# Two-layer S5 and attention trunk: x loaded first, meta tokens turned in two transposes, B's turns between the first matmuls, one angle addition on GpSimd

## The chip, the core and the metric

One core of a Trainium2 chip runs the whole program once. The metric is the device time of that run in microseconds (us), the median of 3 runs for the kernel before; lower is better.

## What is computed

The reference runs 272 tokens (16 learned meta tokens ahead of 256 frames, 2048 wide, float32) through two layers. Layer 0 is an S5 state-space mixer, layer 1 is sliding-window attention, and a squared-ReLU MLP follows each. The change touches only the start of layer 0:

```python
h = concatenate([meta, x], axis=1)                 # 16 + 256 tokens
hn = rms_norm(h, norm_mix_gain[0])
u = hn @ w_in                                      # 2048 -> 1024
dt = exp(log_dt); lam = (a_re + i a_im) * dt
bar = exp(lam)                                     # magnitude and angle
f = (bar - 1) / (a_re + i a_im)
bb = f * (b_re + i b_im)                           # per group: 64 states x 16 channels
bu = einsum('blgc,gpc->blgp', u, bb)
x_t = bar * x_{t-1} + bu_t                         # associative scan over 272 tokens
y = Re(C x) + D * u;  z = gelu(y) * sigmoid(gelu(y) W_glu + b);  h = h + z W_out
```

The kernel runs the scan over chunks of two tokens in rotated coordinates, for which it needs the cosine and sine of 32 x 136 angles on 128 partitions (`cosb`, `sinb`).

## The kernel before, in words

Each engine has a hand-written program, and semaphores order them. TensorE's instructions run in the order in which they are written. The weights stream through a ring of four buffers, and TensorE is the engine that nearly all of the span belongs to. Tokens lie in the free dimension: `h` and `hg` (tokens times gain) are [128, 16, 272], one column block of features for each k.

The start, which is what the change edits:

- SyncE's queue (lines 580 to 613) issues a_re, a_im, log_dt (`prow`, `dtrow`), meta (`ms`, 16 rows), x block 0 (`xs`), the first piece of w_in, x block 1, b_re and b_im (`braw`), the second piece, meta once more as `ms2` (8 x 16 rows of 256), then x blocks 2 and 3 and the rest of w_in. ScalarE's queue (1066 to 1068) issues the identity (`cst`), the first gain and the step constants. GpSimd's queue issues the small vectors and, once x block 1 has landed, 16 loads of C (`craw`, 1357).
- TensorE turns the S5 parameters (660) and the gain (663), does dummy matmuls (`warm_up`, 653), and then goes through `x_unit(n)`, n = 0 to 7 (665 to 678): for each of two k one transpose of meta (675) and two of x (677). Between the units stand `in_first(k, n)` (698 to 706: four float32 matmuls, eight records in the trace, that add 512 rows of w_in to the first 256 columns of u), `b_turn(part)` (16 transposes of 32 x 128, line 686), the turn of the vectors (733) and the bias table's matmul (736), and `c_turn` (695). After `in_half(4)` come `wb_turn(0)` (769: turns of the spread B, `bp`) and three statistics matmuls (778, 780) that need `dssq`; then `in_half(5)` and `wb_turn(1)` to `(3)`, `responses`, and the S5 stage, where `s5_in(i)` (821) waits for `v_read` of the step before.
- ScalarE copies each x unit out, scaled into `hg` (1079) and plain into `h` (1082), squares x and `ms2` for the norm, spreads `bc` into `bp` (1095), makes `dssq` from `roots` (1134, 1135), copies the turned B out (`wb_out`, 1166), and makes sines and cosines (`chunk_angles`, 1156 to 1159).
- VectorE runs `params_1` (from 1420) and `params_2` (to 1533), chains of short operations; `scale` to `bc[0]` and `bc[1]` (1548 to 1550) once both B turns are done; `params_3`; `angle_sums(0)` (1556, 8 of 32 pairs), `angle_wrap(0)` (1564), `angle_sums(1)` (the other 24 pairs); `token_roots` (1581 to 1593, the tokens' inverse roots, signalled as `roots_ready`); `cw[0]`, `rstd` (1613), `u_out(0)`, `angle_wrap(1)`, `cw[1]`; then the scan steps, whose first line is 1633.
- GpSimd, after C's loads: memsets of `bp` (1362) once both B turns are done, of `ca` (1364) once C is turned, and small ones; then `zc` products in the scan (1375).

Of the kernel before, what the change touches and what calls it, by code (L numbers as in the profile page):

```python
# [28 lines left out]
D, NMETA, SEQ = 2048, 16, 256  # L29
# [69 lines left out]
def trunk(nc, x, meta, g_mix, g_mlp, w_in, log_dt, a_re, a_im, b_re, b_im, c_re, c_im, d_skip,  # L99
# [38 lines left out]
    with ctx:  # L138
# [74 lines left out]
        ms = at(A0, "ms", [NMETA, D])  # L213
# [365 lines left out]

        @block.sync  # L580
        def _(sp):
            sp.dma_start(prow[:, 0, :], a_re[0].rearrange("(q g) p -> q (g p)", g=2)).then_inc(sem("par_landed"), 16)
            sp.dma_start(prow[:, 1, :], a_im[0].rearrange("(q g) p -> q (g p)", g=2)).then_inc(sem("par_landed"), 16)
            sp.dma_start(dtrow[:, :], log_dt[0].rearrange("(q g) -> q g", g=2)).then_inc(sem("par_landed"), 16)

# [14 lines left out]
            sp.dma_start(ms[:, :], meta).then_inc(sem("ms_landed"), 16)  # L600
# [46 lines left out]
        def _(pe):  # L647
# [17 lines left out]
            def x_unit(n):  # L665

                if n == 0:
                    pe.wait_ge(sem("ms_landed"), 16)
# [4 lines left out]
                for t in range(2):  # L673
                    k, bank = 2 * n + t, 2 + 2 * (n % 2) + t
                    tr(acc[:, bank, 0:NMETA], ms[:, 128 * k:128 * k + 128], ident[0:NMETA, 0:NMETA])
                    for tb in range(2):
                        m = tr(acc[:, bank, NMETA + 128 * tb:NMETA + 128 * tb + 128],  # L677
                               xs[:, tb, 128 * k:128 * k + 128], ident)
                m.then_inc(sem("x_tr"), 1)

            def b_turn(part):

                pe.wait_ge(sem("b_landed"), 32)
                pe.wait_ge(sem("start_out"), part + 1)
# [13 lines left out]
            def in_first(k, n):  # L698

                pe.wait_ge(sem("hg0_ready"), 2 * k + 2)  # L700
# [7 lines left out]
            def in_half(k):  # L708

                i = k // 2  # L710
                if k == 4:
                    pe.wait_ge(sem("bc_ready"), 1)
                if k == 8:
                    pe.wait_ge(sem("kd_ready"), 1)
# [3 lines left out]
                for t in range(8):  # L718
# [12 lines left out]
            pe.wait_ge(sem("vec_landed"), 16 * 9)  # L731
            pe.wait_ge(sem("par_out"), 1)
            tr(acc[:, 6, 0:NVEC], vrow[:, :], ident[0:NVEC, 0:NVEC]).then_inc(sem("start_tr"), 1)
            pe.wait_ge(sem("bias_in_landed"), 32)
            pe.wait_ge(sem("gain_out"), 1)
            nc.tensor.matmul(acc[0:NH, 7, 0:NREL], tbl[:, :], oh[:, :], start=True,
                             stop=True).then_inc(sem("start_tr"), 1)
# [17 lines left out]
            in_first(3, 1)  # L755
            in_half(4)
# [308 lines left out]
        def _(act):  # L1065
            act.dma_start(cst[:, 0, :], consts[:, 0:128]).then_inc(sem("ident_landed"), 16)
            act.dma_start(vrow[0:KT, :], g_mix[0].rearrange("(a b) -> a b", b=128)).then_inc(sem("gain_landed"), 16)
            act.dma_start(cst[:, 5, 0:56], consts[:, 640:696]).then_inc(sem("steps_landed"), 16)
# [5 lines left out]
            def x_unit(n):  # L1074
# [3 lines left out]
                for t in range(2):  # L1078
                    op = nc.scalar.activation(hg[:, 2 * n + t, :], acc[:, b + t, 0:L], ACT.Copy,
                                              scale=vecs[:, 2 * n + t:2 * n + t + 1])  # L1080
                op.then_inc(sem("hg0_ready"), 1)
                nc.scalar.activation(h[:, 2 * n:2 * n + 2, :], acc[:, b:b + 2, 0:L], ACT.Copy).then_inc(sem("x_out"), 1)
# [30 lines left out]
            act.wait_ge(sem("start_tr"), 1)  # L1113
            nc.scalar.activation(vecs[:, KT:], acc[:, 6, KT:NVEC], ACT.Copy).then_inc(sem("start_out"), 1)
            act.wait_ge(sem("start_tr"), 2)
            nc.scalar.activation(biast[:, :], acc[0:NH, 7, 0:NREL], ACT.Copy).then_inc(sem("start_out"), 1)
            squares(0)
            act.dma_start(cst[:, 2, :], consts[:, 256:384]).then_inc(sem("cst_landed"), 16)
            act.wait_ge(sem("ms2_landed"), 16)
            nc.scalar.activation(ms2[:, :], ms2[:, :], ACT.Square, accum_out=ssqc[:, 4:5])  # L1120
# [59 lines left out]

            act.wait_ge(sem("start_out"), 2)
# [156 lines left out]
        def _(pool):  # L1338
# [13 lines left out]
            pool.wait_ge(sem("x_landed1"), 32)  # L1352
# [46 lines left out]
        def _(dve):  # L1399
# [152 lines left out]
            def angle_sums(k):  # L1552

                q = ANGLE_PART[k]
                n = q.stop - q.start
                tt(cosb[:, q, :].rearrange("p q (a b) -> p q a b", b=8),
                   view(angs[:, q, :], [[25, n], [1, 17], [0, 8]]),
                   view(angs[:, q, 17:18], [[25, n], [0, 17], [1, 8]]), ALU.add).then_inc(sem("angle_sum"), 1)

# [37 lines left out]

            params_1()
            params_2()
# [6 lines left out]
            angle_sums(0)  # L1606
            angle_wrap(0)
            angle_sums(1)
# [353 lines left out]
```

## Time and profile before

| | |
|---|---|
| median of 3 runs | 1953.81 us (1953.21 to 1953.97) |
| the profiled execution, own time | 1950.9 us |
| its span, first to last instruction | 1948.9 us |
| mean granted clock of TensorE | 0.998 |
| busy VectorE / ScalarE / GpSimd | 61% / 46% / 3% |
| the start up to the first scan step | about 55 us |
| the S5 stage behind it | to about 140 us |

A timeline row gives start, duration, engine, line, operation and tiles, with xN where N instructions are merged; idle time ahead of it stands in brackets with what ended it. float32 matmuls show two records each.

### The profile page before, as it was taken

What the parts mean: (1) busy time and instruction counts of PE and PEld (TensorE: products, weight loads), DVE (VectorE), ACT (ScalarE), POOL (GpSimd) and SP (SyncE); (2) the same over time, 40 slices, a digit from 0 to 9 for tenths busy, and PEclk for the clock granted to TensorE, in tenths of its full rate; (3) what the DMA queues carried; (4) which work ended last, traced back from release to release, by engine and by line L of the source; (5) the groups of instructions that cost most, each with busy time, mean ns of one, the idle gap of its engine ahead of it and who ended that gap; (6) DMA issues with size and microseconds to landing.
All of it is one profiled execution on the core that took longest, in us unless ns stands there. A gap on an engine that the chain in (4) does not pass through costs nothing.

```text
span 1948.9 us, 34659 instructions
## 1 busy us (share of the span) xinstructions
PE 1935.9 (99%) x14141; PEld 1789.6 (92%) x14141; DVE 1181.7 (61%) x1293; ACT 889.0 (46%) x1083; POOL 58.0 (3%) x66
## 2 busy tenths in 40 slices
PE   9999999999999999999999999999999999999999
PEld 7889999999999999999998999888888888888887
DVE  8997654545454545454778877655655556465554
ACT  5645443433334433344555665544443434444443
POOL 4220000000000000000000100000000000000000
PEclk9999999999999999999999999999999999999999
DMA  6235686555555555555544445556656565566664
GB/s 175 77 116 185 169 232 176 174 176 175 178 175 173 175 176 178 175 173 174 174 145 145 142 146 180 176 185 189 188 176 200 186 191 189 177 200 178 199 188 152
DMA packets 196731, 338.08 MB, mean 173 GB/s; under 512 B 19544, under 2 KB 38616, under 8 KB 196520
## 3 DMA queue, kind: packets, MB, share of 16 engines
q1 hardware_dynamic: 182616, 332.21, 55.1%
q10 hardware_dynamic: 12896, 2.83, 1.0%
q8 instruction: 111, 1.82, 0.4%
q0 software_dynamic: 1088, 1.06, 0.2%
q14 instruction: 20, 0.16, 0.0%
HBM read 333.48 MB, written 2.14 MB: 172 GB/s over the span
## 4 chain that ended last, share of the span: by engine, by line
PE 94%; DVE 3%; ACT 1%; issue 1%; POOL 0%; DMA 0%; POOLq 0%; SPq 0%; ACTq 0%; DVEq 0%
PE acc L297 51%; PE acc L455 18%; PE acc L414 12%; PE acc L416 6%; PE acc L719 1%; PE acc L703 1%; DVE wlo L279 1%; PE acc L952 0%; PE acc L967 0%; PE acc L980 0%; PE acc L845 0%; PE acc L677 0%; PE acc L985 0%; DVE z L1653 0%; PE acc L653 0%
## 5 line engine op out<-in xcount | busy, mean ns | idle before, releaser
L279 DVE TENSOR_TENSOR wlo<-raw,whi 128x1024 fp32r<-128x1024 f32 x608 | 738.1, 1223 | 576.0 <-ACT whi L274 575.7
L274 ACT ACTIVATE whi<-raw 128x1024 fp32r<-128x1024 f32 x608 | 639.7, 1059 | 906.8 <-PE acc L297 535.7
L414 PE MATMUL acc<-hg,whi 128*128 128x512 f32 x1024 | 359.7, 394 | 0.0
L416 PE MATMUL acc<-hg,wlo 128*128 128x256 f32 x1024 | 288.2, 281 | 0.0
L414 PEld LDWEIGHTS acc<-hg,whi 128*128 128x128 f32 x1024 | 192.4, 188 | 44.8 <-DVE var L364 0.3
L297 PE MATMUL acc<-hg_hi,whi 128*128 128x272 f32 (+1 forms) x1344 | 223.4, 288 | 0.7 <-DVE wlo L279 0.7
L297 PE MATMUL acc<-hg_hi,wlo 128*128 128x272 f32 (+1 forms) x1344 | 221.5, 287 | 0.0
L297 PE MATMUL acc<-hg_lo,whi 128*128 128x272 f32 (+1 forms) x1344 | 221.0, 286 | 0.0
L455 PE MATMUL acc<-whi,a_hi 128*128 128x512 f32 x512 | 202.1, 395 | 0.0
L455 PE MATMUL acc<-wlo,a_hi 128*128 128x512 f32 x512 | 202.1, 395 | 0.0
L455 PE MATMUL acc<-whi,a_lo 128*128 128x512 f32 x512 | 201.1, 393 | 0.0
L416 PEld LDWEIGHTS acc<-hg,wlo 128*128 128x128 f32 x1024 | 192.3, 188 | 0.3
L297 PEld LDWEIGHTS acc<-hg_hi,whi 128*128 128x128 f32 x1344 | 188.3, 188 | 4.3 <-issue 3.0
L297 PE MATMUL acc<-a_hi,wlo 128*128 128x272 f32 x1152 | 191.8, 289 | 0.0
L297 PE MATMUL acc<-a_lo,whi 128*128 128x272 f32 x1152 | 191.2, 288 | 0.0
L297 PE MATMUL acc<-a_hi,whi 128*128 128x272 f32 x1152 | 190.8, 287 | 0.0
L297 PEld LDWEIGHTS acc<-hg_hi,wlo 128*128 128x128 f32 x1344 | 188.0, 188 | 0.0
L297 PEld LDWEIGHTS acc<-hg_lo,whi 128*128 128x128 f32 x1344 | 187.6, 188 | 0.0
L297 PEld LDWEIGHTS acc<-a_hi,whi 128*128 128x128 f32 x1152 | 162.7, 188 | 0.0
L297 PEld LDWEIGHTS acc<-a_hi,wlo 128*128 128x128 f32 x1152 | 162.4, 188 | 0.0
L297 PEld LDWEIGHTS acc<-a_lo,whi 128*128 128x128 f32 x1152 | 162.0, 188 | 0.0
L455 PEld LDWEIGHTS acc<-wlo,a_hi 128*128 128x128 f32 x512 | 96.1, 188 | 22.6
(324 smaller groups left out, 1623.2 us busy)
## 6 DMA issues: line engine op xcount, KB each, us to landing
raw<-in_mlp_w SPq DMA_DIRECT2D x512, 512.0 KB, 3.8
raw<-in_attn_w_qkv SPq DMA_DIRECT2D x40, 512.0 KB, 3.9
raw<-in_attn_w_o SPq DMA_DIRECT2D x32, 512.0 KB, 4.2
raw<-in_s_w_in SPq DMA_DIRECT2D x16, 512.0 KB, 3.9
raw<-in_s_w_out SPq DMA_DIRECT2D x16, 512.0 KB, 4.4
raw<-in_s_w_glu SPq DMA_DIRECT2D x8, 512.0 KB, 3.6
xs<-in_x SPq DMA_DIRECT2D x8, 256.0 KB, 8.4
bias_w<-bias_by_distance ACTq DMA_DIRECT2D x2, 1024.0 KB, 12.5
```

The lines of the kernel that those rows point to most:

```text
L274: nc.scalar.activation(whi[:, k, :, :], raw[:, k, :, :], ACT.Copy).then_inc(sem("hi_split"), 1)
L279: nc.vector.tensor_tensor(wlo[:, k, :, :], raw[:, k, :, :], whi[:, k, :, :], ALU.subtract).then_inc(sem("lo_split"), 1)
L297: m = nc.tensor.matmul(o, w[:, k, t, 128 * n:128 * n + 128], xx[:, kt + t, cols], start=first and t == 0 and j == 0 and not (packed and n ...
L414: nc.tensor.matmul(acc[:, 4 * bset + n, :], whi[:, k, t, cols], hg3[:, :, kt + t, REAL], start=first and t == 0, stop=False, skip_group_ch ...
L416: m = nc.tensor.matmul(acc[:, 4 * bset + n, 0:SEQ], wlo[:, k, t, cols], hg3_hi[:, kt + t, REAL], start=False, stop=last and t == 1, skip_g ...
L455: m = nc.tensor.matmul(acc[:, bank + tb, :], xx[:, 2 * j + t, rows], w[:, k, t, :], start=c > 0 and j == 0 and t == 0 and n == 0, stop=j = ...
L703: m = nc.tensor.matmul(acc[:, IN_BANK[n], 0:L], raw_in(k)[:, t, 128 * n:128 * n + 128], hg[:, 4 * k + t, :], start=k == 0 and t == 0, stop ...
L719: m = nc.tensor.matmul(acc[:, IN_BANK[i], 0:L], raw_in(k % RING, 128)[:, t, :], hg[:, 8 * (k % 2) + t, :], start=k % 2 == 0 and t == 0, st ...
```

## The change

Loads: SyncE issues x block 0 first, and neither meta nor the parameters. ScalarE's queue issues a_re, a_im and log_dt ahead of the identity and the gain, then `ms2`, then the step constants. `ms` and its 16 transposes go; `meta_turn` turns `ms2` in two 128 x 128 transposes ahead of `x_unit(0)`, and VectorE's `meta_columns`, between `params_1` and `params_2`, writes the 16 meta columns of `hg` and `h`. ScalarE copies only the 256 real columns. `in_first(0, n)` waits for those columns.

Order on TensorE: `b_turn(0)` and `b_turn(1)` move ahead, each between two pieces of `in_first`; the vectors' turn and the bias matmul move behind `in_first(3, 1)`, their copies on ScalarE behind `dssq`. GpSimd's C loads wait for x block 2 in place of block 1. `angle_sums(1)` moves from VectorE to GpSimd, between the memsets of `bp` and `ca`.

```diff
@@ sync
-            sp.dma_start(prow[:, 0, :], a_re[0].rearrange("(q g) p -> q (g p)", g=2)).then_inc(sem("par_landed"), 16)
-            sp.dma_start(prow[:, 1, :], a_im[0].rearrange("(q g) p -> q (g p)", g=2)).then_inc(sem("par_landed"), 16)
-            sp.dma_start(dtrow[:, :], log_dt[0].rearrange("(q g) -> q g", g=2)).then_inc(sem("par_landed"), 16)
...
-            sp.dma_start(ms[:, :], meta).then_inc(sem("ms_landed"), 16)
             x_block(0)
             in_weights(0)
...
             in_weights(1)
-            sp.dma_start(ms2[:, :], bass.AP(meta.tensor, meta.offset,
-                                            [[D // 8, 8], [D, NMETA], [1, D // 8]])).then_inc(sem("ms2_landed"), 16)
...
@@ tensor
                 for t in range(2):
                     k, bank = 2 * n + t, 2 + 2 * (n % 2) + t
-                    tr(acc[:, bank, 0:NMETA], ms[:, 128 * k:128 * k + 128], ident[0:NMETA, 0:NMETA])
...
+            def meta_turn():
+
+                pe.wait_ge(sem("ms2_landed"), 16)
+                for t in range(2):
+                    m = tr(acc[:, 1, 128 * t:128 * t + 128], ms2[:, 128 * t:128 * t + 128], ident)
+                m.then_inc(sem("meta_tr"), 1)
...
+                if k == 0:
+                    pe.wait_ge(sem("meta_out"), n + 1)
                 pe.wait_ge(sem("hg0_ready"), 2 * k + 2)
...
             warm_up(6)
+            meta_turn()
             x_unit(0)
             x_unit(1)
             warm_up(6)
             in_first(0, 0)
+            x_unit(2)
             in_first(0, 1)
-            x_unit(2)
             x_unit(3)
...
+            b_turn(0)
             in_first(1, 0)
-            b_turn(0)
+            x_unit(4)
             b_turn(1)
-            x_unit(4)
+            x_unit(5)
             in_first(1, 1)
-            x_unit(5)
+            in_first(2, 0)
             x_unit(6)
-            in_first(2, 0)
+            in_first(2, 1)
             x_unit(7)
-            in_first(2, 1)
             c_turn(0)
             c_turn(1)
...
             in_first(3, 1)
+            pe.wait_ge(sem("vec_landed"), 16 * 9)
+            pe.wait_ge(sem("bias_in_landed"), 32)
+            pe.wait_ge(sem("bc_ready"), 1)
+            tr(acc[:, 7, 352:352 + NVEC], vrow[:, :], ident[0:NVEC, 0:NVEC])
+            nc.tensor.matmul(acc[0:NH, 7, 0:NREL], tbl[:, :], oh[:, :], start=True,
+                             stop=True, skip_group_check=True).then_inc(sem("start_tr"), 1)
             in_half(4)
@@ scalar
+            act.dma_start(prow[:, 0, :], a_re[0].rearrange("(q g) p -> q (g p)", g=2)).then_inc(sem("par_landed"), 16)
+            act.dma_start(prow[:, 1, :], a_im[0].rearrange("(q g) p -> q (g p)", g=2)).then_inc(sem("par_landed"), 16)
+            act.dma_start(dtrow[:, :], log_dt[0].rearrange("(q g) -> q g", g=2)).then_inc(sem("par_landed"), 16)
             act.dma_start(cst[:, 0, :], consts[:, 0:128]).then_inc(sem("ident_landed"), 16)
             act.dma_start(vrow[0:KT, :], g_mix[0].rearrange("(a b) -> a b", b=128)).then_inc(sem("gain_landed"), 16)
+            act.dma_start(ms2[:, :], bass.AP(meta.tensor, meta.offset,
+                                            [[D // 8, 8], [D, NMETA], [1, D // 8]])).then_inc(sem("ms2_landed"), 16)
...
@@ gpsimd
-            pool.wait_ge(sem("x_landed1"), 32)
+            pool.wait_ge(sem("x_landed2"), 32)
...
                 nc.gpsimd.memset(bp[:, k, :, :], 0.0).then_inc(sem("bp_zero"), 1)
+            pool.wait_ge(sem("angle_sum"), 1)
+            angle_sums(tt, 1)
             pool.wait_ge(sem("c_tr"), 2)
             nc.gpsimd.memset(ca[:, :, :, :, :], 0.0).then_inc(sem("ca_zero"), 1)
@@ vector
+            def meta_columns():
+
+                turned = acc[:, 1, 0:256].rearrange("p (t b n) -> p b t n", t=2, b=8)
+                dve.wait_ge(sem("gain_out"), 1)
+                dve.wait_ge(sem("meta_tr"), 1)
+                tt(hg[:, :, 0:NMETA].rearrange("p (b t) n -> p b t n", t=2), turned,
+                   view(vecs[:, 0:KT], [[2, 8], [1, 2], [0, NMETA]]), ALU.mult).then_inc(sem("meta_out"), 1)
+                v.tensor_copy(h[:, :, 0:NMETA].rearrange("p (b t) n -> p b t n", t=2),
+                              turned).then_inc(sem("meta_out"), 1)
+
             params_1()
+            meta_columns()
             params_2()
...
-            angle_sums(0)
+            angle_sums(tt, 0)
             angle_wrap(0)
-            angle_sums(1)
             token_roots()
```

## Rows read from the trace of the kernel before

**Rows 1.** The page, part 1: busy time, share of the span, instructions.

```profile
PE 1935.9 (99%) x14141; PEld 1789.6 (92%) x14141; DVE 1181.7 (61%) x1293; ACT 889.0 (46%) x1083; POOL 58.0 (3%) x66
```

**Rows 2.** Waits of TensorE, 40 to 1948.9 us: total, times, longest (us).

```profile
PE acc L821 <- ACT wb L1166: 0.7, 1, 0.7
```

**Rows 3.** The chain that ended last, 0 to 140 us: start, length, what.

```profile
69.07 3.04 ACT cosb L1159
...
75.02 1.24 PE acc L821 x32
```

**Rows 4.** Timeline of TensorE, 0 to 75 us.

```profile
7.58 0.24 PE L675 MATMUL acc<-cst,ms 16*128 16x16 f32 x1
...
8.12 0.23 PE L675 MATMUL acc<-cst,ms 16*128 16x16 f32 x1
...
11.01 3.94 PE L703 MATMUL acc<-hg,raw 128*128 128x272 f32 x16
...
20.26 3.71 PE L686 MATMUL acc<-cst,braw 32*128 32x32 f32 x32
...
24.79 3.65 PE L703 MATMUL acc<-hg,raw 128*128 128x272 f32 x8
...
43.83 1.04 PE L769 MATMUL acc<-cst,bp 128*128 128x128 f32 x8
44.70 0.61 PE L778 MATMUL acc<-dssq,cst 128*128 128x128 f32 x4
```

**Rows 5.** Stretches: busy PE, PEld, DVE, ACT, POOL; granted clock, DMA share, GB/s.

```profile
25.00:30.00 5.00, 5.00 (x18) 3.20 (x17) 4.93 (x5) 1.85 (x5) 2.58 (x2) 0.69 0.60 134
```

**Rows 6.** Timeline of ScalarE, 0 to 75 us (ACTq: its DMA issues).

```profile
1.70 0.45 ACTq L1068 DMA_DIRECT2D cst<-in_consts  x1
...
42.94 0.29 ACT L1135 ACTIVATE dssq<-cst,roots 16x16 f32<-16x16 f32 x1
```

**Rows 7.** DMA issues at 0.76 us: KB, us from issue to landing.

```profile
cst<-in_consts ACTq DMA_DIRECT2D x1, 64.0 KB, 2.0
```

**Rows 8.** The same for the issue at 17.86 us.

```profile
cst<-in_consts ACTq DMA_DIRECT2D x1, 64.0 KB, 8.0
```

**Rows 9.** Timeline of VectorE, 0 to 90 us.

```profile
4.75 0.26 DVE L1414 COPY prm<-acc 128x96 f32<-128x96 f32 x1 [0.68 <-PE acc L660]
...
20.35 0.18 DVE L1533 SCALAR_TENSOR_TENSOR prm<-prm,cst 128x32 f32<-128x32 f32 x1
24.07 1.23 DVE L1548 TENSOR_TENSOR bc<-acc,prm 128x1024 f32<-128x1024 f32 x1 [3.54 <-PE acc L686]
...
32.24 1.29 DVE L1556 TENSOR_TENSOR cosb<-angs 128x1088 f32<-128x1088 f32 x1
...
34.78 3.55 DVE L1556 TENSOR_TENSOR cosb<-angs 128x3264 f32<-128x3264 f32 x1
...
38.51 1.42 DVE L1587 TENSOR_SCALAR roots<-roots 128x3 f32<-128x3 f32 x1
...
42.22 1.22 DVE L1548 TENSOR_TENSOR cw<-cc,prm 128x1024 f32<-128x1024 f32 x1
...
55.18 1.29 DVE L1633 TENSOR_TENSOR rot<-acc,cosb 128x1088 f32<-128x1088 f32 x1 [0.90 <-PE acc L821]
```

**Rows 10.** Timeline of GpSimd, 0 to 80 us.

```profile
16.69 4.78 POOL L1357 DMA_DIRECT2D craw<-in_s_c_im  x8
...
36.39 3.52 POOL L1364 MEMSET ca<- 128x4096 f32 x1 [8.81 <-PE acc L695]
...
63.34 2.52 POOL L1375 TENSOR_TENSOR zc<-z,cosb 128x1088 f32<-128x1088 f32 x1 [23.36 <-DVE zs L1667]
```

**Rows 11.** Timeline of GpSimd in the attention stage.

```profile
1049.85 1.04 POOL L1393 TENSOR_TENSOR pnw<-e_sb,small 128x512 f32<-128x512 f32 x1 [8.82 <-DVE small L1806]
```

**Rows 12.** Timeline of VectorE, 1039 to 1052 us.

```profile
1041.41 0.69 DVE L1813 TENSOR_TENSOR pnw<-e_sb,small 128x512 f32<-128x512 f32 x1
...
1050.07 1.38 DVE L1813 TENSOR_TENSOR pnw<-e_sb,small 128x512 f32<-128x512 f32 x1
```

More of the change, by code:

```diff
@@ L578, in u_count, with angle_sums @@
             return max(i, 1)
+        def angle_sums(add, k):
+            q = ANGLE_PART[k]
+            n = q.stop - q.start
+            add(cosb[:, q, :].rearrange("p q (a b) -> p q a b", b=8),
+                view(angs[:, q, :], [[25, n], [1, 17], [0, 8]]),
+                view(angs[:, q, 17:18], [[25, n], [0, 17], [1, 8]]), ALU.add).then_inc(sem("angle_sum"), 1)
         @block.sync
         def _(sp):
-            sp.dma_start(prow[:, 0, :], a_re[0].rearrange("(q g) p -> q (g p)", g=2)).then_inc(sem("par_landed"), 16)
-            sp.dma_start(prow[:, 1, :], a_im[0].rearrange("(q g) p -> q (g p)", g=2)).then_inc(sem("par_landed"), 16)
-            sp.dma_start(dtrow[:, :], log_dt[0].rearrange("(q g) -> q g", g=2)).then_inc(sem("par_landed"), 16)
             def x_block(b):
@@ L665, in x_unit @@
             def x_unit(n):
-                if n == 0:
-                    pe.wait_ge(sem("ms_landed"), 16)
                 if n % 2 == 0:
@@ L679, in x_unit @@
                 m.then_inc(sem("x_tr"), 1)
+            def meta_turn():
[3 more added lines that the diff above has]
+                m.then_inc(sem("meta_tr"), 1)
             def b_turn(part):
                 pe.wait_ge(sem("b_landed"), 32)
-                pe.wait_ge(sem("start_out"), part + 1)
+                if part:
+                    pe.wait_ge(sem("gain_out"), 1)
+                else:
+                    pe.wait_ge(sem("par_out"), 1)
                 for c in range(GCH):
@@ L712, in in_half @@
                     pe.wait_ge(sem("bc_ready"), 1)
+                if k == 6:
+                    pe.wait_ge(sem("start_out"), 2)
                 if k == 8:
@@ L727, in _ @@
             in_first(0, 0)
+            x_unit(2)
             in_first(0, 1)
-            x_unit(2)
             x_unit(3)
[L731 to L737, printed above, removed]
+            b_turn(0)
             in_first(1, 0)
-            b_turn(0)
+            x_unit(4)
             b_turn(1)
-            x_unit(4)
+            x_unit(5)
             in_first(1, 1)
-            x_unit(5)
+            in_first(2, 0)
             x_unit(6)
-            in_first(2, 0)
+            in_first(2, 1)
             x_unit(7)
-            in_first(2, 1)
             c_turn(0)
@@ L1078, in x_unit @@
                 for t in range(2):
-                    op = nc.scalar.activation(hg[:, 2 * n + t, :], acc[:, b + t, 0:L], ACT.Copy,
+                    op = nc.scalar.activation(hg[:, 2 * n + t, REAL], acc[:, b + t, REAL], ACT.Copy,
                                               scale=vecs[:, 2 * n + t:2 * n + t + 1])
                 op.then_inc(sem("hg0_ready"), 1)
-                nc.scalar.activation(h[:, 2 * n:2 * n + 2, :], acc[:, b:b + 2, 0:L], ACT.Copy).then_inc(sem("x_out"), 1)
+                nc.scalar.activation(h[:, 2 * n:2 * n + 2, REAL], acc[:, b:b + 2, REAL], ACT.Copy).then_inc(sem("x_out"), 1)
             def turns(src, dst_half, dst_full, ready, done):
@@ L1112, in _ @@
             x_unit(3)
[L1113 to L1116, printed above, removed]
             squares(0)
+            act.wait_ge(sem("meta_tr"), 1)
+            nc.scalar.activation(ms2[:, :], ms2[:, :], ACT.Square, accum_out=ssqc[:, 4:5])
             act.dma_start(cst[:, 2, :], consts[:, 256:384]).then_inc(sem("cst_landed"), 16)
-            act.wait_ge(sem("ms2_landed"), 16)
-            nc.scalar.activation(ms2[:, :], ms2[:, :], ACT.Square, accum_out=ssqc[:, 4:5])
             for n in range(4, 8):
@@ L1179, in responses_out @@
                 op.then_inc(sem("kd_ready"), 1)
+            act.wait_ge(sem("start_tr"), 1)
+            nc.scalar.activation(vecs[:, KT:], acc[:, 7, 352 + KT:352 + NVEC], ACT.Copy).then_inc(sem("start_out"), 1)
+            nc.scalar.activation(biast[:, :], acc[0:NH, 7, 0:NREL], ACT.Copy).then_inc(sem("start_out"), 1)
             act.wait_ge(sem("start_out"), 2)
@@ L1550, in scale @@
                 tt(dst[:, :, :, :], dst[:, :, :, :], btmp[:, :, :, :], ALU.add).then_inc(sem(done), 1)
[L1552 to L1558, printed above, removed]
             def angle_wrap(k):
```

1 line of the change is left out of this document (removed).

## The prediction

> **What bounds the kernel now.** I read the shares of the page first: TensorE is busy 99% of the span, the others far less [rows 1]. Then TensorE's waits after 40 us, of which the one shown is typical: each is under 1 us, so a microsecond won or lost at the start is hardly absorbed later [rows 2]. The chain that ended last runs on TensorE up to about 50 us, passes to ScalarE's work up to the cosines at 69 to 72 us, and returns to TensorE at the state matmuls at 75 us [rows 3]. So two things set the end: when TensorE gets through the first 50 us, and when the ScalarE and VectorE chains that hang on the same steps get through. The timelines of the start tell which of them is last at each step; the reader should look for the point where TensorE changes from giving orders to waiting for them.
>
> The sum is made against the profiled execution (span 1948.9 us, own time 1950.9). The median of the runs is 1953.8, 2.9 us above it, and a difference in span is added to the median. 0.2% of it, 3.9 us, is taken as what a measurement can tell from no change.
>
> **TensorE, what it wins.** An x unit costs twice the 0.54 us between two meta transposes, 1.08 us [rows 4]. Without the meta transpose between them, I price x transposes at those of B's spread, 1.04 us for 8 less the pipeline's tail, 0.11 us each [rows 4]: 0.44 us for four. Eight units win 8 x 0.63 = 5.0 us; the two transposes of `ms2` cost 0.3. The bound on the other side is that the x transposes keep the present pace and only the 16 meta ones go, less than 16 x 0.24 = 3.8 us [rows 4]. One piece of `in_first` took 3.65 us against 1.97 (half of the 3.94 for two) at a granted clock of 0.69 over its stretch, at the low level of 1.2 GHz for most of it, right behind the 32 small B transposes [rows 4, 5]. B's turns are now split by large matmuls, so I take that fall as gone: 1.5 us more. Vectors and bias are moved only. TensorE's own work ahead of the statistics then shrinks by some 6 us, and is ready for them at about 40.7 us, allowing for a later start and a half microsecond of wait for the squares, instead of 44.7 [rows 4].
>
> **The first loads.** The third load on ScalarE's queue was issued at 1.70 us and took 0.45 [rows 6], so the identity, now fourth, is issued at 2.15 instead of 0.76. It landed in 2.0 us in the quiet start [rows 7]; the same 64 KB on the same queue took 8.0 us behind SyncE's backlog [rows 8]. With only x block 0 and a piece of w_in in front I take 2.9 us, nearer to the quiet end, and keep both: it lands at 5.0 (4.15 to 10.15). It had landed 2.0 us ahead of VectorE's copy of the turned parameters at 4.75 [rows 9] and was not what that waited for; now it is, and with half a microsecond of transposes between, the copy moves 0.9 us later (0 to 6). x landing earlier wins nothing by itself, since unit 0 stands behind these transposes, six dummy matmuls and `ms2`.
>
> The Trainium skill, DMA: Bandwidth & Descriptors, section on issuing engines, says that issuing from several engines saves only issue time and that all loads share the same engines. By that rule the identity could be as late as the 8.0 us row has it; the row bears out that direction, and the sum would be by it up to 5 us worse.
>
> **VectorE up to B.** `params_2` ended at 20.53 us (20.35 + 0.18 [rows 9]). Add 0.9 for the start and two operations of `meta_columns` with 256 elements, a quarter of 1.23 us [rows 9] and some fixed part, 0.4 each: 22.2. B's second turn: the first matmuls began at 11.01 [rows 4]; now they wait for the meta columns and the later x units, say 11.4. From there to the second B turn stand three pieces of 1.97, three x units of 0.44 and 3.7 us of B transposes, 10.9 us: 22.3. Both agree, so `scale` starts at 22.3 instead of 24.07 [rows 9]: 1.8 us won. Call this start s. GpSimd's C loads took 0.6 us each (4.78 for 8 [rows 10]); 16 of them behind x block 2 (about 17 us), the sink load and the `bp` memsets end at about 31, just ahead of s + 9.5. `bp_zero` was never last and still is not.
>
> **The addition on GpSimd, where the forecast turns.** It takes 3.5 us off VectorE (3.55 [rows 9]) and should, alone, let `token_roots` start 3.5 us sooner. Two rows speak against it. VectorE's product of two SBUF tiles took 1.38 us instead of 0.69 when it started 0.22 us after a GpSimd product of 1.04 us [rows 11, 12]: it stood still until GpSimd had finished. And `token_roots`' first TENSOR_SCALAR on 3 elements took 1.42 us and ended at 39.93, when GpSimd's memset of `ca` ended at 39.91 [rows 9, 10]. So either kind of VectorE operation is held by a running GpSimd instruction, of its length.
>
> Now the working. `angle_sums(0)` began 8.17 us behind s and took 1.29 [rows 9]; it ends at s + 9.5. `angle_wrap(0)`, another 1.2 us, gets in first: s + 10.7. GpSimd's addition has 3264 elements, three times the 1088 of the `zc` product of 2.52 us [rows 10]: 7.6 us (5.5 if it went at the pace of a cheaper form, 8.5 if slower), to s + 18.3. VectorE waits. Behind it GpSimd starts the 3.52 us memset of `ca` at once, since C has long been turned, while VectorE has two short operations ahead of its TENSOR_SCALAR; that one is held again, to s + 21.8. From there to the roots it was 2.3 us (39.93 to 42.22 [rows 9]): s + 24.1 = 46.4, against 42.2. ScalarE's `dssq` ended 1.0 us behind the roots [rows 6, 9]: 47.4. The statistics matmuls then begin at 47.45, not 44.70 [rows 4]: **2.75 us later**, although TensorE was there at 40.7.
>
> The Trainium skill, SBUF — State Buffer, section "Who interferes with whom", gives a rule for it: an operation of VectorE with two SBUF inputs and a GpSimd one that reads SBUF exclude each other, whichever starts first holds the other for its whole length, and a GpSimd instruction that only writes holds up VectorE's two-port forms alone. The trace agrees with both halves (1.38 against 0.69 us, and 1.42 us for 3 elements). By the rule VectorE's `scale` to `bc[1]` next to the `bp` memsets costs nothing, and if GpSimd gets in ahead of `angle_wrap(0)` the order changes; that is a rival below.
>
> **The clock.** TensorE stands idle from about 40.7 to 47.4. The granted clock fell before even behind small transposes [rows 4, 5], so a fall in this gap is likely, and the next work, `in_half(5)`, lies straight on the chain. A low stretch cost 1.7 us at most in one piece [rows 4]; some of it will lie in the idle time, so I take **1.0 us** (0 to 2.5).
>
> **What follows.** VectorE's chain: roots 4.2 us late, and 0.9 us of idle time ahead of the first scan step [rows 9] takes some of it back, so that it is about 3.4 late. `angle_wrap(1)` finds its sum finished. ScalarE's chain to the cosines hangs on `wb_turn`, so it is late as TensorE is. All three are close to 2.75 + 1.0 = 3.75, which I round to 3.8: 1953.8 + 3.8 = **1957.6 us**. Behind 75 us nothing is changed.
>
> **The rivals.**
> *The clock costs nothing or the full price.* Nothing: +2.8, 1956.6. A full stretch in busy time, or two: +5.0.
> *GpSimd gets in first.* Its addition runs from s + 9.5 to s + 17.1, the memset of `ca` runs beside `angle_wrap(0)`, and the roots come at s + 22.9, 1.2 us sooner: +2.6, 1956.4. For it speaks only that both are released by the same semaphore.
> *GpSimd does not hold VectorE.* Then the roots come at about 36 us, TensorE arrives first with the statistics at 40.7 and keeps its win: 4.0 us faster, 1949.8. Against it stand the rows above; it would need an addition of short operations that let VectorE in between.
> *Slower: `ms2` at the head.* `meta_turn` stands ahead of every x unit. `ms2` is issued at about 3.1 us; if it lands 8.0 us later [rows 8], at 11.1, instead of by 8.5 when the dummy matmuls are done, units, `in_first` and both B turns move by 2.6 us, s to 24.9, and the sum is +6.4: 1960.2. It decides from 8.5 us on, microsecond for microsecond. For it: the 8.0 us row; against it: at 3 us the backlog is still small.
> *The addition is quicker,* 5.5 us: 2 us less, 1955.6.
>
> **How the numbers follow.** Forecast as worked out, between +2.9 and +5.5: 0.45, of which 0.25 above 3.9. Clock free 0.12, clock at full price 0.05 (slower). GpSimd first 0.12. `ms2` or the identity late 0.12 (slower). Quicker addition 0.06. No hold 0.08, half of it beyond 3.9. Slower: 0.25 + 0.05 + 0.12 = 0.42; faster 0.04, with a little more for what I have not seen, 0.07; same 0.51. The range must leave out no more than 0.2: from 1952.5 (leaving out the case without a hold) to 1961.0. The cases of one sign hold most of it.
>
> **What would show it.** In the new trace: x transposes 0.11 us apart; no low clock at 25 us; `scale` to `bc[0]` at 22.3; GpSimd's addition at about 7.6 us, next to one VectorE operation of `token_roots` on 2 elements that lasts as long, and then a TENSOR_SCALAR of about 3.4 us; TensorE idle for 5 to 7 us ahead of line 778's successor, waiting for `dssq`; a granted clock below 1 around 45 to 50. I am wrong if VectorE's short operations run at their 0.2 us beside the addition, or if `meta_turn` waits.

## The result and the profile after

| | before | after |
|---|---|---|
| median of 7 runs each, us | 1953.97 | 1962.14 |
| lowest and highest | 1953.13, 1956.68 | 1960.83, 1963.58 |
| span of the profiled execution | 1948.9 | 1960.7 |
| first scan step on VectorE starts | 55.18 | 66.31 |

The change makes the kernel slower: 1962.14 over 1953.97 is a ratio of 1.004 (95% interval 1.0031 to 1.0049), 8.2 us. The forecast was 3.8 us, with the range's upper end at 1961.0. Between the two profiled executions lie 11.8 us and between the medians 8.2, because the profiled execution of before lay 3.1 us under this median and that of after 0.6 over its own; the spans of single executions of one kernel differ by some microseconds here, and the costs below are therefore taken from medians wherever a run has one. Four executions that took over 6% longer than the rest of their kernel (two of before, one each of the kernels with the parameters' loads alone and with the dummy matmuls) are left out of every median.

I read the page's first lines, to see whether any engine's work grew.

```profile
span 1960.7 us, 34632 instructions
PE 1936.0 (99%) x14127; PEld 1791.5 (91%) x14127; DVE 1187.0 (61%) x1294; ACT 888.4 (45%) x1083; POOL 64.5 (3%) x67
```

TensorE has 14 instructions fewer and the same busy time as in [rows 1], in a span 11.8 us longer. So the difference is idle time of TensorE; the busy time is only equal because some matmuls of the start ran slower and took back what the dropped transposes saved. TensorE's timeline of the start (start, duration, engine, line, operation, idle time ahead of it) shows where:

```profile
8.69 0.53 PE L660 MATMUL acc<-cst,prow 32*128 32x32 f32 x3 [5.55 <-DMA cst<-in_consts]
...
13.74 0.69 PE L682 MATMUL acc<-cst,ms 128*128 128x128 f32 x2 [1.00 <-DMA ms<-in_meta_tokens]
...
18.24 2.00 PE L712 MATMUL acc<-hg,raw 128*128 128x272 f32 x8
20.07 0.60 PE L674 MATMUL acc<-cst,xs 128*128 128x128 f32 x4
...
29.59 3.83 PE L712 MATMUL acc<-hg,raw 128*128 128x272 f32 x16
...
37.63 1.07 PE L702 MATMUL acc<-cst,craw 128*128 128x128 f32 x8 [1.51 <-ACT h L1098]
...
52.88 1.19 PE L789 MATMUL acc<-dssq,cst 128*128 128x128 f32 x4 [4.70 <-issue]
...
54.54 6.08 PE L730 MATMUL acc<-hg,raw 128*128 128x272 f32 x16
```

Four things stand in it. TensorE waits 5.55 us for the identity, which in before was there when the parameters were (its turn of them began at 4.21). It waits 1.00 for `ms2`. It waits 1.51 for ScalarE's last copy of an x unit ahead of the turn of C. And it stands still for 4.70 us ahead of the statistics, which start at 52.88 instead of 44.70 [rows 4]; the piece of `in_half(5)` behind them takes 6.08 us for 16 records, where `in_half(4)` took 3.93. From the start of the statistics to the end of that piece it is 7.58 us (52.88 to 60.46). The landing of the first loads, from the view of DMA issues in the first 4 us (KB each, us from issue to landing), against 2.0 us for the identity in [rows 7]:

```profile
cst<-in_consts ACTq DMA_DIRECT2D x1, 64.0 KB, 6.5
...
dtrow<-in_s_log_dt ACTq DMA_DIRECT2D x1, 0.2 KB, 5.3
```

The idle time of 4.70 is said to be "issue": the profile has no semaphore event for it. On the chain that ended last (start, length, what) it and the load of `ms2` are the two long steps that do no work:

```profile
3.20 10.50 DMA ms<-in_meta_tokens
...
48.19 4.70 issue
```

ScalarE's timeline explains it: the first `dssq` waits for VectorE's `roots` until 51.89.

```profile
51.89 0.69 ACT L1146 ACTIVATE dssq<-cst,roots 128x128 f32<-128x128 f32 x2 [7.22 <-DVE roots L1602]
```

VectorE's timeline up to the first scan step, and under it GpSimd's:

```profile
9.26 0.26 DVE L1431 COPY prm<-acc 128x96 f32<-128x96 f32 x1 [2.06 <-PE acc L660]
...
14.54 0.42 DVE L1612 TENSOR_TENSOR hg<-acc,vecs 128x256 f32<-128x256 f32 x1 [0.71 <-PE acc L682]
14.88 0.41 DVE L1614 COPY h<-acc 128x256 f32<-128x256 f32 x1
...
29.27 1.23 DVE L1565 TENSOR_TENSOR bc<-acc,prm 128x1024 f32<-128x1024 f32 x1 [2.63 <-PE acc L693]
...
39.97 5.97 DVE L1592 TENSOR_TENSOR roots<-ssqc 128x2 f32<-128x2 f32 x1
...
46.03 3.44 DVE L1596 TENSOR_SCALAR roots<-roots 128x3 f32<-128x3 f32 x1
...
51.77 1.22 DVE L1565 TENSOR_TENSOR cw<-cc,prm 128x1024 f32<-128x1024 f32 x1
...
66.31 1.29 DVE L1652 TENSOR_TENSOR rot<-acc,cosb 128x1088 f32<-128x1088 f32 x1 [2.48 <-PE acc L832]
```

```profile
38.81 7.11 POOL L583 TENSOR_TENSOR cosb<-angs 128x3264 f32<-128x3264 f32 x1 [6.04 <-DVE cosb L583]
45.86 3.51 POOL L1381 MEMSET ca<- 128x4096 f32 x1
```

An operation on 2 elements takes 5.97 us and one on 3 elements 3.44. The first ends at 45.94, when GpSimd's addition does (45.92), the second at 49.47, when its memset does (49.37). Both short operations end with the GpSimd operation beside them: VectorE stood still while GpSimd ran. Last the stretches behind the statistics (busy times by engine, then the granted clock):

```profile
50.00:55.00 5.00, 2.12 (x7) 1.88 (x8) 4.66 (x13) 2.69 (x7) 0.00 (x0) 0.71 0.08 23
55.00:60.00 5.00, 5.00 (x15) 3.76 (x14) 4.96 (x5) 3.04 (x3) 0.00 (x0) 0.61 0.00 0
```

The granted clock is 0.61 where TensorE is busy all the time: near the low level of 1.2 GHz for most of the stretch, right behind the gap.

### The profile page after: what moved, and what is told of

Its sections match the earlier page's. It is cut to its first block, busy times and chain, and to the rows that moved or that the text cites. A ratio compares the mean times of both kernels' runs of the same rounds, so it can differ in the third digit from the quotient of the medians.

```text
span 1960.7 us, 34632 instructions
## 1 busy us (share of the span) xinstructions
PE 1936.0 (99%) x14127; PEld 1791.5 (91%) x14127; DVE 1187.0 (61%) x1294; ACT 888.4 (45%) x1083; POOL 64.5 (3%) x67
## 4 chain that ended last, share of the span: by engine, by line
PE 93%; DVE 3%; ACT 2%; DMA 1%; issue 1%; ACTq 0%; SPq 0%; DVEq 0%
PE acc L296 51%; PE acc L454 18%; PE acc L413 12%; PE acc L415 6%; PE acc L730 1%; PE acc L712 1%; DMA raw<-in_mlp_w 1%; DMA ms<-in_meta_tokens 1%; DVE wlo L278 0%; PE acc L991 0%; PE acc L963 0%; PE acc L978 0%; PE acc L996 0%; PE acc L856 0%; DVE z L1672 0%
```

## The experiments

Two causes are in question: the first loads, and the addition on GpSimd. The first five kernels undo or do one or both. Each ratio is to runs of the kernel before on the same chip in the same session, whose median was 1952.98 us for four of these five, 1953.28 for the parameters' loads alone and the three kernels behind them, and 1953.66 for the last two.

### The parameters' loads back at the head, identity first

```diff
@@ sync, scalar (on the changed kernel)
-            act.dma_start(prow[:, 0, :], ...) and a_im, log_dt, ahead of the identity
+            sp.dma_start(prow[:, 0, :], ...) and a_im, log_dt, ahead of x_block(0)
```

> The changed kernel with the load order of before: a_re, a_im and log_dt first on SyncE's queue, the identity first on ScalarE's; meta still only as ms2 on ScalarE's queue; the addition stays on GpSimd. Theory (two costs, the late identity and the hold by GpSimd): the parameters' copy is back at 4.8 us from 9.3, the first scale at 22 to 23 from 29.3, the statistics matmuls at about 46 from 52.9, the hold of about 6 + 3.4 us stays: 6 to 7 us faster than the changed kernel, still 2 to 4 us slower than before. Rival (the loads alone): equal to or faster than before, by up to 4 us. Rival (the addition alone): no gain over the changed kernel.

1955.77 us against 1952.98, ratio 1.0015 (1.0006 to 1.0025). The identity landed in 1.9 us and `bc[0]` started at 22.61. VectorE and TensorE:

```profile
33.31 5.96 DVE L1592 TENSOR_TENSOR roots<-ssqc 128x2 f32<-128x2 f32 x1
```

```profile
46.20 1.01 PE L792 MATMUL acc<-dssq,cst 128*128 128x128 f32 x4 [4.68 <-issue]
```

The hold, the gap of 4.7 us and a slow `in_half(5)` (4.97 us) stay, 6.7 us earlier. This run has almost the state that I had forecast, in which `bc[0]` starts at 22.3: the forecast had the statistics at 47.45 and the sum at +3.8; it shows 46.20 and +2.8.

### The addition back on VectorE

```diff
@@ vector, gpsimd (on the changed kernel)
             angle_wrap(0)
+            angle_sums(tt, 1)
             token_roots()
...
-            pool.wait_ge(sem("angle_sum"), 1)
-            angle_sums(tt, 1)
```

> The changed kernel with angle_sums(1) back on VectorE behind angle_wrap(0). Theory: no hold, roots at about 46 from 51.8 us, TensorE not idle ahead of the statistics at 48, no low clock in in_half(5) (3.9 us, not 6.1): about 7 us faster than the changed kernel, 0 to 2 us slower than before. Rival (the loads alone): no more than 1 us faster than the changed kernel. Rival (the addition alone): as fast as before or faster, by up to 4 us.

1953.8 us, ratio 1.0004 (0.9994 to 1.0014): no difference from before that can be told. The wait for the identity is as long (5.52 us), but the operations of `token_roots` take 0.14 to 0.17 us each and TensorE goes straight from `wb_turn` into the statistics:

```profile
46.33 0.61 PE L789 MATMUL acc<-dssq,cst 128*128 128x128 f32 x4
```

### Both back

The two edits together; what is left of the change are x ahead of meta, the two transposes of `ms2`, and the orders on TensorE and ScalarE.

> The changed kernel with both undone: what is left is the meta turn by two transposes, B's turns sooner and vectors later. Theory: statistics at about 41 us against 44.7 of before, so 4 us faster than before. Rival (the shorter x units and moved turns win nothing, since something else is last): within 1 us of before.

1947.47 us, ratio 0.9975 (0.9965 to 0.9985). TensorE's statistics come 4.0 us earlier than in [rows 4] (40.74 against 44.70), and the next piece of `in_half` takes 3.93 us:

```profile
40.74 0.61 PE L792 MATMUL acc<-dssq,cst 128*128 128x128 f32 x4
```

So the rest of the change is a gain of 5.5 us in the medians. The two profiled executions show 4.0 us of it (3.8 in their spans); where the other 1.5 lie isn't shown, and the profile of before was 2.1 us under that median of before (1952.98), this one 0.6 under its own. Putting the loads as in the change on top of it costs 1953.8 - 1947.47 = 6.3 us; putting the addition on top of it costs 1955.77 - 1947.47 = 8.3. Together -5.5 + 6.3 + 8.3 = +9.1, and the changed kernel has +8.2: the two costs add up to within a microsecond.

### The addition alone, on the kernel before

```diff
@@ gpsimd, vector (on the kernel before)
                 nc.gpsimd.memset(bp[:, k, :, :], 0.0).then_inc(sem("bp_zero"), 1)
+            pool.wait_ge(sem("angle_sum"), 1)
+            angle_sums(tt, 1)
...
             angle_wrap(0)
-            angle_sums(1)
```

> The kernel before with nothing but the long angle addition moved to GpSimd. Theory: VectorE stands still for about 6 us beside the addition and 3.4 beside the memset of ca, the statistics come at about 47.7 instead of 44.7 us: 3 us slower than before, 5 if the clock falls in the gap. Rival (GpSimd does not hold VectorE, or it is hidden): within 1 us of before or up to 3 us faster.

1958.25 us, ratio 1.0031 (1.002 to 1.0043): 5.3 us slower. VectorE's two held operations are there without anything else of the change, and the statistics wait 4.51 us, to 51.33. (This execution lay 1.9 us above its median: its first matmuls ran slower, and `in_first` began at 13.68 instead of 11.01. The roots come 22.5 us behind `bc[0]`, as in the changed kernel.)

```profile
39.10 5.29 DVE L1585 TENSOR_TENSOR roots<-ssqc 128x2 f32<-128x2 f32 x1 [0.59 <-ACT xs L1115]
...
44.48 3.44 DVE L1589 TENSOR_SCALAR roots<-roots 128x3 f32<-128x3 f32 x1
```

It costs 3.0 less than on top of the other gains. An explanation that fits is that in before TensorE reached the statistics 4 us later anyway.

### The parameters' loads alone, on the kernel before

```diff
@@ sync, scalar (on the kernel before)
-            sp.dma_start(prow[:, 0, :], ...) and a_im, log_dt, first on SyncE's queue
+            act.dma_start(prow[:, 0, :], ...) and a_im, log_dt, ahead of the identity
```

> The kernel before with nothing but a_re, a_im and log_dt moved from SyncE's queue to ScalarE's, ahead of the identity. Theory: the identity lands at 6 to 9 us instead of 2.8, and the head of TensorE's order (parameters, dummy matmuls, x units) moves by 2 to 5 us: 2 to 5 us slower than before. Rival (a load's place on its own queue is all that counts): the identity lands at 4.2, nothing moves, within 1 us of before.

1956.94 us, ratio 1.0019 (1.0009 to 1.003): 3.7 us slower between medians, from three loads of 16, 16 and 0.2 KB that change the queue. TensorE:

```profile
7.12 0.52 PE L657 MATMUL acc<-cst,prow 32*128 32x32 f32 x3 [3.97 <-DMA cst<-in_consts]
```

The identity landed in 4.9 us, 1.6 sooner than in the changed kernel, whose SyncE queue begins with x and not with meta. The profiled execution lay 3.4 us above its median, with slow matmuls at 25 and 33 us (8 records in 3.79 and 3.83 us), so I read only the landing from it and the price from the medians.

### The memset of `ca` ahead of the addition

```diff
@@ gpsimd (on the changed kernel)
+            pool.wait_ge(sem("c_tr"), 2)
+            nc.gpsimd.memset(ca[:, :, :, :, :], 0.0).then_inc(sem("ca_zero"), 1)
             pool.wait_ge(sem("angle_sum"), 1)
             angle_sums(tt, 1)
-            pool.wait_ge(sem("c_tr"), 2)
-            nc.gpsimd.memset(ca[:, :, :, :, :], 0.0).then_inc(sem("ca_zero"), 1)
```

> The changed kernel with GpSimd's memset of ca ahead of the angle addition. Theory (any gap between two VectorE operations lets the waiting GpSimd instruction in, and it holds for its whole length): the memset ends at about 42, the addition runs from there to 49, the roots come at 51 to 52 us as in the changed kernel: within 1 us of it. Rival (the second hold, 3.4 us, is paid only because the memset follows the addition): 3 us faster than the changed kernel.

1961.41 us, ratio 1.0039 (1.0025 to 1.0054). GpSimd, then VectorE:

```profile
37.31 3.52 POOL L1379 MEMSET ca<- 128x4096 f32 x1 [5.98 <-PE acc L702]
40.87 6.00 POOL L583 TENSOR_TENSOR cosb<-angs 128x3264 f32<-128x3264 f32 x1
```

```profile
38.51 0.15 DVE L1592 TENSOR_TENSOR roots<-ssqc 128x2 f32<-128x2 f32 x1
...
39.43 1.41 DVE L1596 TENSOR_SCALAR roots<-roots 128x3 f32<-128x3 f32 x1
40.88 6.11 DVE L1598 TENSOR_SCALAR roots<-roots 128x3 int32<-128x3 int32 x1
```

The memset lets the TENSOR_TENSOR on 2 elements pass in 0.15 us, but holds the first TENSOR_SCALAR from 39.43 to its own end. The roots come 21.3 us behind `bc[0]`, 1.2 sooner than in the changed kernel, which is too little for these intervals to tell. That the memset is over early helps so little for this reason: `token_roots` is a chain of operations of 0.15 us with a gap behind each, GpSimd's addition starts in the first gap (40.87), and the next operation, on 3 elements, is held until 46.99. The addition takes 6.00 us here and 7.11 in the changed kernel, where VectorE's `angle_wrap(0)`, 1.29 us from 38.76, was running when it started. So it was itself held for about 1.1 us, and its own length is 6.0. The head of this kernel is that of the changed kernel to the letter, with the identity as late (the parameters' turn began at 8.69 in both).

### TensorE kept busy ahead of the statistics

```diff
@@ tensor (on the changed kernel)
             wb_turn(0)
+            pe.wait_ge(sem("cc_out"), 2)
+            for _ in range(20):
+                nc.tensor.matmul(acc[:, 5, 0:128], warm[:, :], warm[:, :], start=True, stop=True)
             pe.wait_ge(sem("ones_made"), 1)
```

> The changed kernel with 20 dummy matmuls (4.5 us) in TensorE's idle time ahead of the statistics matmuls. Theory (the clock falls because TensorE stands idle): statistics start as before at about 53 us, in_half(5) takes 3.9 us instead of 6.1, the granted clock stays at 2.4 GHz: 2 to 3 us faster than the changed kernel. Rival (the low clock has another cause): in_half(5) stays at 6 us and the time unchanged.

1962.25 us, ratio 1.0043 (1.0027 to 1.0059): not faster than the changed kernel. The piece behind the statistics is, though, as the timeline of TensorE shows; and then, 16 us later, there is a new gap and a slow stretch:

```profile
48.80 4.63 PE L787 MATMUL acc<-warm 128*128 128x128 f32 x40
53.65 0.68 PE L792 MATMUL acc<-dssq,cst 128*128 128x128 f32 x4 [0.22 <-issue]
...
54.58 3.94 PE L730 MATMUL acc<-hg,raw 128*128 128x272 f32 x16
...
69.82 0.86 PE L835 MATMUL acc<-u,wb 32*128 32x136 f32 x17 [1.72 <-issue]
70.62 9.29 PE L730 MATMUL acc<-hg,raw 128*128 128x272 f32 x32
```

3.94 us instead of 6.08, at a granted clock of 1.00: the gap was what the slow piece came from. The other kernels agree: `in_half(5)` took 4.97 to 6.44 us in the four with a gap of 3.5 to 4.7 us ahead of the statistics, and 3.93 or 3.94 in those without. With the statistics matmuls, which were slow too, it cost 2.95 us in the profile of after (7.58 against 4.63 with the addition back). The first scan step starts at 64.63 instead of 66.31, although the identity took 7.3 us in this execution and the statistics began 0.8 later. But 32 records at 70.62 take 9.29 us (twice 3.94 would be 7.9), in a stretch of 68 to 76 us whose granted clock is 0.79, behind a pause of 1.72 us. In this execution the gain was given back; whether it is in all, the nearly equal medians suggest but don't show. What the pause of 1.72 us came from isn't shown.

### The turn of C later, on top of both back

```diff
@@ tensor (on the kernel with both back)
+            in_first(3, 0)
             c_turn(0)
             c_turn(1)
-            in_first(3, 0)
```

> The changed kernel with both costs undone (loads of before, addition on VectorE), and besides C's turns behind in_first(3, 0), so that TensorE does not wait 1.5 us for ScalarE's last copy of h. Theory: that wait goes, the statistics then wait some 0.6 us for dssq: about 1 us faster than the version with both undone, 6 to 7 us faster than before. Rival (ScalarE's chain through the later cc copies is last): no gain over that version.

1946.96 us, ratio 0.9969 (0.9956 to 0.9981), 0.5 below the kernel with both back (0.8 if each is taken from before of its own session), which is within the noise. The wait of 1.51 us for ScalarE becomes one of 0.93 ahead of `in_first(3, 0)`: it too needs ScalarE's copies of `x_unit(7)`, right behind which it now stands, so the new order moves the wait and hides little of it. In before `in_first(2, 1)` stood between that unit and the turn of C; that order wasn't tried. It is the fastest of these kernels, 0.3% under before.

### Why the identity is late: its place in the queue, or what SyncE had issued

Both on the kernel with the addition back on VectorE (1953.8, 0.8 above before of its session; these two are of another session). First, the identity ahead of the parameters on ScalarE's queue:

```diff
@@ scalar
+            act.dma_start(cst[:, 0, :], consts[:, 0:128]).then_inc(sem("ident_landed"), 16)
             act.dma_start(prow[:, 0, :], ...)
...
-            act.dma_start(cst[:, 0, :], consts[:, 0:128]).then_inc(sem("ident_landed"), 16)
```

> The kernel with the addition back on VectorE (1953.8 us, identity issued at 2.16 us as the fourth load of ScalarE's queue and landed at 8.66) with one edit: the identity is issued first on that queue, at about 0.77, and a_re, a_im and log_dt behind it. Theory L1 (a load is late by what SyncE's queue had issued before it: 1 MB of x and w_in by 2.2 us): the identity is issued together with SyncE's first x load and lands by 3.5; log_dt, now issued at about 2.2, lands 5 us or more after it, at 7.3 to 8, and VectorE's copy of the turned parameters, which waits for both, gains at most 1.3 us on 9.2 (8 to 9). The gain in time is 0.5 to 1.5 us. Theory L2 (what counts is the three loads ahead in its own queue): the identity lands by 3.0, the parameters lose only 0.5 us each (log_dt by 5.8 to 7.5), the copy starts by 6.5 and the time falls by 2.5 to 4 us.

1954.35 us against 1953.66, ratio 1.0004 (0.9994 to 1.0014): nothing gained. DMA issues, then VectorE:

```profile
cst<-in_consts ACTq DMA_DIRECT2D x1, 64.0 KB, 5.0
...
dtrow<-in_s_log_dt ACTq DMA_DIRECT2D x1, 0.2 KB, 6.1
```

```profile
8.30 0.21 DVE L1426 COPY prow<-dtrow 32x128 f32<-32x128 f32 x1 [7.09 <-DMA dtrow<-in_s_log_dt]
```

Issued at 0.77, with nothing ahead of it on its queue and SyncE's first x load issued at 0.75, the identity still took 5.0 us, where 3.5 had been the latest that I expected. log_dt, now fourth, took 6.1 us for 0.2 KB, and the parameters' turn went at 8.66, as before this edit. The identity itself landed 2.9 us sooner than without the edit (5.77 against 8.66), so this run alone doesn't show what the kernel would do with all the small loads sooner. And another load would have stood in the way:

```profile
13.66 0.44 PE L682 MATMUL acc<-cst,ms 128*128 128x128 f32 x2 [1.54 <-DMA ms<-in_meta_tokens]
```

`ms2` landed at 13.61, and no x unit goes before it. In all five profiled kernels that begin with x and have `ms2` behind the parameters and the identity, it took 10.1 to 10.6 us and was the last load that TensorE waited for ahead of the x units. Second, SyncE's x waits instead:

```diff
@@ sync
+            sp.wait_ge(sem("ident_landed"), 16)
             x_block(0)
```

> The kernel with the addition back on VectorE, with one edit: SyncE issues its first x load only when the identity has landed; the order on ScalarE's queue stays a_re, a_im, log_dt, identity. Theory L1 (SyncE's 1 MB ahead delays it): with nothing of SyncE's under way the identity lands in 1.9 to 2.6 us after its issue at 2.16, at about 4.5, log_dt in about 2 us, the parameters' turn goes at about 4.6; the x loads are issued 3.8 us later, and x unit 0 goes at about 11 us instead of 10, so that the time is within 2 us of 1953.8. Theory L2 (own queue): the identity still takes 4.5 to 6.5 us, and everything is 4 to 7 us later.

1950.36 us, ratio 0.9979 (0.997 to 0.9989): 3.3 us faster than before, 4.0 faster than the kernel above in the same session, 3.4 faster than the one without the wait in the other session, and more than the 2 us that I had allowed, although x is issued 3.3 us later.

```profile
cst<-in_consts ACTq DMA_DIRECT2D x1, 64.0 KB, 1.9
```

```profile
4.12 0.52 PE L661 MATMUL acc<-cst,prow 32*128 32x32 f32 x3 [0.97 <-DMA cst<-in_consts]
...
8.84 1.26 PE L675 MATMUL acc<-cst,xs 128*128 128x128 f32 x8 [0.50 <-DMA xs<-in_x]
```

Behind three loads of its own queue and issued at 2.15, the identity landed in 1.9 us. So the three loads ahead of it cost only issue time, and the rest of its lateness is what SyncE issues around it, 1 MB of x and w_in by 2.2 us, and more behind the identity. `ms2`, issued at 3.11, was not waited for at all (its turn went at 7.71, right behind the dummy matmuls). x itself was waited for 0.50 us. That x comes first won nothing and took 4.3 us from the statistics (42.02 here against 46.33). The parameters at the head of SyncE's queue are still the better order, 5.5 us under before of their session against 3.3.

## Why the prediction was wrong

**What bounds the kernel.** Right, and it carried: what the start loses arrives at the end. From the first scan step to the end of the span it is 1893.7 us in before and 1894.4 in after.

**TensorE, what it wins.** Right. Four x transposes take 0.44 us from start to start (20.07 to 20.51), the price that I gave them, and the low clock at 25 us is gone (a granted clock of 1.00 from 22 to 35 us, 16 records of `in_first` in 3.83 us). The case "no hold" put this gain at 4.0 us with the late copy's 0.9 in it, so 4.9 without; with both causes removed it is 5.5. My terms don't add up to that 4.0, though: 5.0 - 0.3 + 1.5, less 0.9 for the start and 0.5 for the squares, is 4.8, and TensorE would have been ready at 39.9 and not 40.7. The forecast doesn't hang on it, since there the statistics waited for the roots. One cost is missing in my working. The change puts `x_unit(7)` right ahead of the turn of C, which waits for ScalarE's two copies of that unit (0.84 and 0.60 us one behind the other); in before `in_first(2, 1)` lay between them. That is the wait of 1.51 us, and the new order and the durations of the copies were there to read.

**The first loads.** This is the step that failed: the term for the late start, 0.9 us, for which I priced the identity's landing near the quiet row and left `ms2` out of the sum. I took 2.9 us for the identity's landing, "nearer to the quiet end", with 8.0 us as the other end; it was 6.5, nearer to the other. The kernel's own row of 8.0 us was the better analogue: the backlog of SyncE's queue is what counts, and it is there from the first x load on. The copy of the parameters started at 9.26, not 5.65, 3.6 us late, and TensorE was late with it, since all its work begins with the identity. Behind it came `ms2`, which I had as a rival with the argument that "at 3 us the backlog is still small"; by 3.2 us SyncE had issued 1.5 MB, and `ms2` took 10.50 us, from 3.20 to 13.70. 1.00 us of that was still waited for behind the late identity. By my own rule (from 8.5 us on, microsecond for microsecond) it would have cost 5.2 us even with the identity in time, so the two delays lie over each other, and by this rule putting only the identity right would have won little. On top of that the dummy matmuls and the x transposes between `ms2` and `in_first` ran 1.4 us slower in this execution (13.74 to 18.24, 4.50 us) than in the one with the addition back (13.34 to 16.48, 3.14 us). That is no property of the change: the kernel with the memset first has the same head, and took 3.14 us too. Together `in_first` started at 18.24 and not at 11.4. From there to `bc[0]` I had 10.9 us, and it was 11.03: s = 29.27 instead of 22.3. In the medians the loads cost 6.3 us, where my sum has 0.9. That difference of 5.4 is more than the whole miss of 4.5 (1962.14 - 1957.6).

The rule of the Trainium skill that I weighed there (DMA: Bandwidth & Descriptors, section "Issuing engines are not separate DMA queues": another engine's queue saves issue time only, the engines behind it are shared) agrees with the last two experiments: 5.0 us with the best place in the queue, 1.9 with the worst place and nothing large under way. It pointed to the right end, and I gave it as a sentence on the side.

**VectorE up to B.** `meta_columns` cost 0.42 and 0.41, as said (0.4 each).

**The addition on GpSimd.** The mechanism was right, in its order too: `angle_wrap(0)` got in first, the addition ran beside one operation on 2 elements, the memset beside one TENSOR_SCALAR of 3.44 us. Its size was a little too large: forecast to s + 18.3, it ended at s + 16.65, and the roots were there at s + 22.5 and not s + 24.1. My price of 7.6 us came from three `zc` products of 2.52; the addition's own length is 6.0. In the medians the hold costs 8.3 us; my sum has 3.8 + 4.0 = 7.8 between the case without a hold and the forecast. That the two are so close is partly luck: the hold was 1.6 us shorter than forecast, and the clock cost more. The rival without a hold is refuted by five kernels, and "GpSimd first" by the order in the trace.

**The clock.** Forecast 1.0 us (0 to 2.5); in the profile of after the statistics and the piece behind the gap took 2.95 us longer, beyond the upper end, and in that of the kernel with the loads back 1.7 (6.29 us from 46.20 to 52.49). The gap itself was shorter than forecast, 4.7 us and not 6.7, and in the changed kernel it came later, since TensorE was late to it as well. What the clock costs in the median is open, since filling the gap moved the slow stretch and not the median.

**The sum.** Stated in terms of medians: gain 4.9 against 5.5 measured, loads 0.9 against 6.3, hold 7.8 (clock included) against 8.3; 3.8 against 9.1, of which the interaction leaves 8.2. One term was wrong by a factor of seven. The range was too narrow by 1.1 us, because the late identity and the late `ms2` shared one case of 0.12, though 8.0 us was written down as a bound beside 2.0.

## What to carry to other kernels

When a small load decides when the first engine can start, look at how much the other queues have issued ahead of it, not at its place in its own: here 64 KB took 1.9 to 2.1 us with nothing large under way, and 4.9 to 7.3 beside the first megabyte, and holding the large loads back until the small one had landed made the kernel 3.4 to 4.0 us faster. Look too for the next load in line: behind the late identity an even later `ms2` would have held the same work. Don't give GpSimd a long operation beside a chain of short VectorE operations on which another engine waits: here the chain had a gap behind each of its operations, GpSimd started in the first one, and a 0.15 us operation then lasted as long as GpSimd's. And where two ends of a bound lie far apart, name the row that has the same mechanism (a backlog on another queue), and not the one that has the nearer time.

## What the runs showed of the hardware

- A GpSimd addition with two SBUF inputs held both kinds of VectorE operation that came during it, a TENSOR_TENSOR of 2 elements (5.97 us) and even a TENSOR_SCALAR with one input of 3 elements (6.11 us). A memset on GpSimd held the TENSOR_SCALAR (3.44 us) but neither a TENSOR_TENSOR of 2 elements (0.15 us) nor `angle_wrap(0)` with its two SBUF inputs (1.29 us, its usual time), both beside the memset of `ca` in the kernel with the memset first. The hold goes both ways: GpSimd's addition was 1.1 us longer when it started in a VectorE operation (7.11 against 6.00). The Trainium skill (SBUF — State Buffer, "Who interferes with whom") counts `tensor_scalar` among the operations that can take a two-port mode, which contends with any GpSimd instruction, lets an operation with two SBUF inputs contend only with a GpSimd one that reads SBUF, and says that whoever issues first keeps the other out for its whole length; these numbers agree.
- The float32 addition on GpSimd takes 6.00 us for 3264 elements per partition, 1.8 ns each, where VectorE took 3.55 for the same addition [rows 9]: 1.1 ns each.
- A load of 0.2 KB is not spared by a backlog: log_dt landed in 4.0 to 6.1 us in the six profiled kernels that issue it on ScalarE's queue beside SyncE's x (64 KB took 4.9 to 7.3 there), against 1.8 to 2.1 where nothing large was under way.
- TensorE's first dozen dummy matmuls ran at half the later pace, 12 in 2.93 us in before and after alike, against 1.50 for the second dozen in before and 2.47 in after, though the granted clock of these stretches reads 1.00. The eight x transposes between the two dozens took 1.92 us in after and 1.04 in the kernel with the memset first, whose head is the same. So at the start the pace of equal instructions tells what that column doesn't; that it is the clock that changes there isn't shown.
